# A projection slab moved between the channel transposes, the state product put first on GpSimd, and decays picked from split cumulative sums in a transformer-and-SSD kernel

## What is computed

```python
xbc = jax.nn.silu(causal_depthwise_conv(xbc, conv_w[l], conv_b[l]))
xs, bs, cs = jnp.split(xbc, [SSD_D_INNER, SSD_D_INNER + SSD_GROUPS * SSD_STATE], axis=-1)
dt = jax.nn.softplus(dt_raw + dt_bias[l]);  A = -jnp.exp(a_log[l])
...
x = xh * dt;  a_cs = jnp.cumsum(dt * A)
seg = a_cs[:, :, :, None] - a_cs[:, :, None, :]
decay = jnp.exp(jnp.where(causal, seg, -jnp.inf))
cb = jnp.einsum('bclgn,bcsgn->bclsg', Cc, Bc)
y_diag = jnp.einsum('bclsg,bclsgr,bcsgrp->bclgrp', cb, decay, x)
states = jnp.einsum('bclgn,bclgr,bclgrp->bcgrpn', Bc, decay_to_end, x)
y_off = jnp.einsum('bclgn,bcgrpn,bclgr->bclgrp', Cc, prev, jnp.exp(a_cs))
...
merged = sigmoid(gate_a) * (y_attn @ w_attn_branch[l]) + sigmoid(gate_b) * (y_ssd @ w_ssd_branch[l])
```

## Time and profile before

| | |
|---|---|
| median of 3 runs | 1382.62 us (1381.84 to 1382.67) |
| profiled execution, its own time | 1379.86 us |
| its span on the core | 1378.1 us |
| TensorE matmuls busy | 1324.7 us, 96% |
| weight loads (PEld) busy | 1206.4 us, 88% |
| VectorE, ScalarE, GpSimd busy | 944.8, 766.2, 205.6 us |
| mean granted clock of TensorE | 0.988 of full |

### The profile page before, as it was taken

One profiled execution on the slowest core, in us unless ns is written; L12 is line 12 of the kernel. 1 busy time (PEld: TensorE's weight loads), 2 busy tenths in 40 slices (PEclk: granted clock), 3 DMA queues, 4 the chain that ended last, 5 costly groups with the idle time before them and its releaser, 6 DMA issues.

```text
span 1378.1 us, 23083 instructions
## 1 busy us (share of the span) xinstructions
PE 1324.7 (96%) x9022; PEld 1206.4 (88%) x9022; DVE 944.8 (69%) x1369; ACT 766.2 (56%) x1150; POOL 205.6 (15%) x165
## 2 busy tenths in 40 slices
PE   9999999999989999999999998989999999999998
PEld 8999989889989999988998887979999788777876
DVE  6555575486566555566687775765666799999996
ACT  5333346565545333366465775325645677777774
POOL 1222220030001222210301313410001000202020
PEclk9999999999999999999999999999998999999999
DMA  8655544522356555544543442315455599999991
GB/s 311 212 187 186 186 142 157 183 93 93 131 156 197 183 183 184 171 135 154 184 148 123 123 154 71 100 47 180 143 169 184 212 400 365 339 367 334 370 338 52
DMA packets 73943, 263.44 MB, mean 191 GB/s; under 512 B 8320, under 2 KB 9600, under 8 KB 73728
## 3 DMA queue, kind: packets, MB, share of 16 engines
q1 hardware_dynamic: 72864, 260.39, 55.5%
q10 hardware_dynamic: 992, 1.86, 0.4%
HBM read 261.17 MB, written 1.05 MB: 190 GB/s over the span
## 4 chain that ended last, share of the span: by engine, by line
PE 69%; DVE 9%; ACT 5%; issue 2%; POOL 1%; DVEq 0%; ACTq 0%; POOLq 0%
PE bank L561 21%; PE bank L563 20%; PE bank L562 20%; DVE sb_wlo L518 3%; DVE sb_wlo L505 2%; ACT sb_Uh L636 1%; PE bank L2782 1%; PE bank L653 1%; ACT sb_aw L1729 1%; PE bank L2839 1%; DVE sb_XC L2118 1%; PE bank L741 1%; ACT sb_whi L489 0%; POOL sb_Xe L2441 0%; ACT sb_XC L1762 0%
## 5 line engine op out<-in xcount | busy, mean ns | idle before, releaser
L505 DVE TENSOR_TENSOR sb_wlo<-sb_raw,sb_whi 128x1024 fp32r<-128x1024 f32 (+2 forms) x304 | 384.0, 1308 | 166.3 <-ACT sb_whi L489 166.1
L489 ACT ACTIVATE sb_whi<-sb_raw 128x1024 fp32r<-128x1024 f32 (+3 forms) x308 | 301.9, 1030 | 227.8 <-PE bank L563 221.7
L561 PE MATMUL bank<-sb_Uh,sb_whi 128*128 128x256 f32 x1216 | 348.8, 287 | 11.5 <-DVE sb_wlo L505 4.3
L562 PE MATMUL bank<-sb_Ul,sb_whi 128*128 128x256 f32 x1216 | 345.3, 284 | 0.0
L563 PE MATMUL bank<-sb_Uh,sb_wlo 128*128 128x256 f32 x1216 | 345.1, 284 | 0.0
L561 PEld LDWEIGHTS bank<-sb_Uh,sb_whi 128*128 128x128 f32 x1216 | 234.1, 192 | 16.6 <-issue 9.2
L562 PEld LDWEIGHTS bank<-sb_Ul,sb_whi 128*128 128x128 f32 x1216 | 234.2, 193 | 0.9
L563 PEld LDWEIGHTS bank<-sb_Uh,sb_wlo 128*128 128x128 f32 x1216 | 234.2, 193 | 0.0
L561 PE MATMUL bank<-sb_whi,sb_Uh 128*128 128x256 f32 (+3 forms) x560 | 161.1, 288 | 7.1 <-DVE sb_Ul L645 5.3
L563 PE MATMUL bank<-sb_whi,sb_Ul 128*128 128x256 f32 (+3 forms) x560 | 158.5, 283 | 0.0
L562 PE MATMUL bank<-sb_wlo,sb_Uh 128*128 128x256 f32 (+3 forms) x560 | 158.5, 283 | 0.0
(11 more groups left out here) (407 smaller groups left out, 2258.5 us busy)
## 6 DMA issues: line engine op xcount, KB each, us to landing
sb_raw<-in_slabs SPq DMA_DIRECT2D x162, 512.0 KB, 4.5
sb_raw<-in_ffn_in SPq DMA_DIRECT2D x88, 512.0 KB, 4.5
sb_raw<-in_moe_in SPq DMA_DIRECT2D x50, 512.0 KB, 5.7
sb_raw<-in_ffn_out SPq DMA_DIRECT2D x44, 512.0 KB, 3.9
sb_raw<-in_moe_out SPq DMA_DIRECT2D x26, 512.0 KB, 5.8
sb_deep_free<-in_moe_in SPq DMA_DIRECT2D x16, 512.0 KB, 5.9
sb_deep_uh<-in_moe_in SPq DMA_DIRECT2D x16, 512.0 KB, 5.2
sb_deep_ul<-in_moe_in SPq DMA_DIRECT2D x16, 512.0 KB, 6.3
```

Of the source, the lines that this page charges most:

```text
L489: nc.scalar.activation(whi[:, i % NSLOT, c], raw[:, i % NSLOT, c], ACT.Copy).then_inc(S("hi_done"), 1)
L505: nc.vector.tensor_tensor(wlo[:, i % NSLOT, c], raw[:, i % NSLOT, c], whi[:, i % NSLOT, c].bitcast(F32), ALU.subtract).then_inc(S("lo_done ...
L561: pe.matmul(o, lh, rh, start=start, stop=False, skip_group_check=True)
L562: pe.matmul(o, lh, rl, start=False, stop=False, skip_group_check=True)
```

## The change

The six parts, as the code has them:

1. Decays. VectorE spreads dt*A over a tile DTR with the 32 heads four times side by side; two matmuls with `upto` (new, `cst_mm`) give the cumulative sums with heads along the partitions, four copies of them, in bank 4. VectorE casts them to fp32r (CST) and turns the second and fourth copy into the remainder. Rows 0 to 63 and rows 64 to 127 each hold high and low part of all heads. A decay row is now one fp32r matmul of 64 rows: a 0/1 column PICKR, spread over 128 columns, times CST. The two banks' matmuls alternate between the row halves.
2. The slab of u = 0 goes between the second and third block of transposes (`side(0)`), B's transposes go ahead of the blocks, and inside the loop pass u now has slab u + 1 (up to u = 4).
3. ScalarE casts slab wa2 after the third Silu, and makes the decays `ee` before the XS copies; BTM is copied after two of them.
4. VectorE does the remainder of that slab before `fe`.
5. GpSimd starts a unit when its own two blocks of XS are there, and makes Xe before Xd.
6. Xd, Xe and BTM no longer share their place with XC.

```diff
+        ("pick", (np.arange(P)[:, None] % SH == np.arange(SH)[None, :]) * 1.0),
...
+                    hi_upto("wa0")
...
             act.activation(ssm[:, 9], ssm[:, 5], ACT.Exp).then_inc(S("ee"), 1)
-            hi_upto("wa0")
+            for j in range(8):
+                if j == 2:
+                    act.wait_ge(*reach("bt_tr", 1))
+                    act.activation(BTM[:].rearrange("p g n -> p (g n)"), bank[4][:, :], ACT.Copy).then_inc(S("bt_ev"), 1)
+                act.wait_ge(*reach("xs_tr", j + 1))
+                act.activation(XS[:, :, j * 256:(j + 1) * 256], tok(j % 4, 256), ACT.Copy).then_inc(S("xs_ev"), 1)
...
+            side_out(0)
             for u in range(8):
-                if u < 6:
-                    hi_upto(f"wa{u}" if u < 4 else f"g{u}")
+                if u < 5:
+                    hi_upto(f"wa{u + 1}" if u < 3 else f"g{u + 1}")
...
-                if u < 6:
-                    side_out(u)
+                if u < 5:
+                    side_out(u + 1)
...
+                    dve.tensor_copy(DTR[:], ssm[:, 2:4].unsqueeze(2).to_broadcast([P, NT, P // SH, SH])).then_inc(S("dt_d"), 1)
...
+            dve.tensor_copy(PICKR[:], const("pick")).then_inc(S("cst"), 1)
+            dve.wait_ge(*reach("cst_mm", 1))
+            dve.tensor_copy(CST[:], bank[4][:, 0:T]).then_inc(S("cst"), 1)
+            dve.wait_ge(*reach("cst", 2))
+            for r in (SH, 3 * SH):
+                dve.tensor_tensor(CST[r:r + SH, :], bank[4][r:r + SH, 0:T], CST[r:r + SH, :].bitcast(F32), ALU.subtract).then_inc(S("cst"), 1)
...
+            lo_upto("wa0")
             dve.wait_ge(*reach("ee", 1))
             dve.tensor_tensor(ssm[:, 7], ssm[:, 7], ssm[:, 0], ALU.mult).then_inc(S("fe"), 1)
-            lo_upto("wa0")
...
-                pool.wait_ge(*reach("xs_ev", 8))
+                pool.wait_ge(*reach("xs_ev", 2 * g + 2))
...
+            claim(4, "cst", 4)
+            for t in range(NT):
+                last = pe.matmul(bank[4][:, t * P:(t + 1) * P], DTR[:, t].rearrange("p a h -> p (a h)"), const("upto"),
+                                 start=t == 0, stop=True, skip_group_check=True)
+            last.then_inc(S("cst_mm"), 1)
...
+            xs_turn(0)
+            xs_turn(1)
+            pe.wait_ge(*reach("dsa_olo", 8))
+            side(0)
+            for j in range(2, 8):
+                xs_turn(j)
             for u in range(9):
...
-                        for h in range(4):
-                            col = ssm[:, 2 + t, 8 * g + 4 * k + h:8 * g + 4 * k + h + 1].to_broadcast([P, P])
-                            last = pe.matmul(bank[n % 4][:, h * P:(h + 1) * P], col, const("upto"), start=h == 0, stop=True,
-                                             skip_group_check=True)
+                    for h in range(4):
+                        for k in range(2):
+                            rows, hd = slice(64 * k, 64 * k + 64), 8 * g + 4 * k + h
+                            last = pe.matmul(bank[(2 * u + k) % 4][:, h * P:(h + 1) * P], PICKR[rows, hd:hd + 1].to_broadcast([64, P]),
+                                             CST[rows, t * P:(t + 1) * P], start=h == 0, stop=True, skip_group_check=True)
...
-                    if u < 6:
+                    if u < 5:
+                        side(u + 1)
```

More of the change, by code:

```diff
@@ L348, in two_blocks @@
             pad = sb("pad", [P, P], F32, p2)
+            CST = sb("CST", [P, T], F32R, p2)
+            PICKR = sb("PICKR", [P, SH], F32R, p2)
+            DTR = sb("DTR", [P, NT, P // SH, SH], F32, p2)
+            Xd = sb("Xd", [P, 2, 512], F32, p2)
+            Xe = sb("Xe", [P, 512], F32, p2)
+            BTM = sb("BTM", [P, SG, SN], F32, p2)
             with ExitStack() as pa:
@@ L359, in two_blocks @@
                 ST = sb("ST", [P, SG, 512], F32, pa)
-                Xd = sb("Xd", [P, 2, 512], F32, pa)
-                Xe = sb("Xe", [P, 512], F32, pa)
-                BTM = sb("BTM", [P, SG, SN], F32, pa)
             with ExitStack() as pa:
@@ L1764, in _ @@
                     gate2_out(3)
-            for j in range(8):
-                act.wait_ge(*reach("xs_tr", j + 1))
-                act.activation(XS[:, :, j * 256:(j + 1) * 256], tok(j % 4, 256), ACT.Copy).then_inc(S("xs_ev"), 1)
-            act.wait_ge(*reach("bt_tr", 1))
-            act.activation(BTM[:].rearrange("p g n -> p (g n)"), bank[4][:, :], ACT.Copy).then_inc(S("bt_ev"), 1)
+                    hi_upto("wa0")
             act.preload_act_table(ACT.Exp)
@@ L2205, in _ @@
                     t, g = divmod(u, 4)
-                    if u < 6:
-                        lo_upto(f"wa{u}" if u < 4 else f"g{u}")
+                    if u < 5:
+                        lo_upto(f"wa{u + 1}" if u < 3 else f"g{u + 1}")
                     for k in range(2):
@@ L2721, in _ @@
             gate2(3)
-            pe.wait_ge(*reach("dt_d", 2))
+            pe.wait_ge(*reach("dt_d", 3))
             claim(5, "acs", 1)
@@ L2737, in _, with side, xs_turn @@
                 last.then_inc(S("cb_mm"), 1)
-            for j in range(8):
+            def side(u):
+                s_ = need(f"wa{u}" if u < 4 else f"g{u}")
+                claim(7, "side_ev", u + 1)
+                src = (OAh, OAl) if u < 4 else (Uh, Ul)
+                by_feature(s_, 7, *src, KD, 256).then_inc(S("slab_used"), 1)
+            def xs_turn(j):
                 pe.wait_ge(*reach("xc", 3 + j // 2))
```

22 lines of the change are left out of this document (10 added, 12 removed).

## The result

| | before | after |
|---|---|---|
| median of 5 runs (lowest to highest) | 1382.67 us (1381.84 to 1387.41) | 1374.99 us (1374.81 to 1376.87) |
| profiled execution, its span | 1379.86, 1378.1 us | 1376.87, 1375.1 us |
| first cumulative sum, z0, the stretch between | 823.84, 918.79, 94.95 us | 829.93, 912.07, 82.14 us |

The ratio is 0.9943, 95% interval [0.9925, 0.9961]: 0.6% faster, 7.7 us. 1366.0 was forecast, in a range of 1361 to 1373, and the measured time lies above it. The sign was right, the size half of what was said.

A forecast was written before the change was run, and what follows sets the result against it. TensorE, busy 96% of the span, bounds the kernel, apart from its waits and low clock. Decays 8.5, waits 6.2, clock 2.3 and added work -0.45 make 16.6 us saved: 1366.0 us, range 1361.0 to 1373.0.

The forecast's parts named there:

- The end: Loop's last three passes: waits for VectorE of 1.6, 2.6 and 2.8 us, low clock only for the last 4.86 us.
- the end gives it back: Rival: clock falls at the first of three end waits, costing 4 to 5 us; saving 12, 1370.6 us; chance 0.10.
- my 78.36: Forecast length in us from the first cumulative sum, 823.84, to slab z0's start, 902.2; before, 94.95.
- At nothing: Items put at no cost: the DTR copy in the top-k rounds, the loads, 32 more constant columns, everything behind z0.
- The wait for Xe and the slow stretch behind it: Before the first state product: wait of 4.7 us goes, and 5.1 us at low clock with it, worth 2.3 us.
- ST comes late once: Pass 1: TensorE waits 0.9 us because bank 6 is emptied late and ST's copy ends only at 845.7.
- The move itself: Slab wa0 among the transposes really runs earlier; the rival that it is held up: about 7 saved, 1375.6 us, chance 0.04.
- the decay pass: Each of eight decay passes on TensorE: 0.70 us instead of 1.76, saving 8.5 us in all, bounds 4.8 and 10.5.
- the nearest row: Trace row behind the 0.70 us: 64-row weight loads on alternating halves, starting about 0.05 us apart.
- my estimate of 0.86 us: Decay pass by the skill's formula: eight weight loads of 107 ns; the sum would then save 1.3 us less.
- what the decays are worth: Shorter decays on TensorE's line: 8 x (1.76 - 0.70) = 8.5 us saved, added sums costing 0.45.
- longer waits of the end: Waits for VectorE in the loop's last three passes, within the 7.9 us of waits left after the change.

The follow-up runs named there:

- warm-end run: Kernel after, plus matmuls on zeros before the three waits for VectorE's bank-6 product at the loop's end: 1368.95 us, ratio 0.9891.
- best version: Kernel after, with VectorE's bank-6 product placed earlier and 8 matmuls on zeros behind the product with ST: 1365.28 us; with the constants table not widened, 1364.74.
- S alone: Kernel before, with only the slab moved among the transposes and the copies made earlier; old decays, Xd first: 1377.01 us, ratio 0.9964.
- D alone: Kernel before, with only the new 64-row fp32r decays and their transposed sums: 1388.36 us, ratio 1.0036.
- D with S: Kernel after, with GpSimd making Xd before Xe again, so new decays and moved slab only: 1384.50 us, ratio 1.0005.
- X: GpSimd making Xe before Xd; as the only edit to the kernel before: 1376.40 us, ratio 0.9959.
- the first run above: Kernel before, unchanged, run and traced again as a control: 1383.44 us, ratio 1.0001.

## Why the prediction was right and wrong

The miss is 1374.99 - 1366.0 = 9.0 us. Two steps failed, and each is measured by a run that undoes it.

**"The end", 4.5 us.** The step "TensorE's line: ... last bank-6 product at 897.3, and from there 4.86 us at the low clock as today" put the fall at the last of three waits. It came at the first, and the rival "the end gives it back" is what happened, down to its size: 4 to 5 us forecast, 3.9 in the stretch (82.21 against my 78.36), some 1.2 in z0, where the clock is low for 4.8 us instead of the 2.3 of the first trace before, and 4.5 in the warm-end run. I gave it 0.10 on one trace, in which the clock had held through 2.62 us. The same program run again let it fall there. Of four traces with the old end (the kernel before twice, and with 32 and 64 unread columns) the clock held past the first wait in two and fell in it or right behind it in two; in all five traces with the change's end and without zeros (first waits of 2.43 and once 1.52 us) it fell there. One execution did not carry that step; without other traces the rival deserved about the forecast's chance.

**"At nothing", about 3 us.** "The 32 further constant columns ride on one early load" looked at the transfer alone. The columns move tiles, and the matmuls that read them go from 227.8 to 232.3 ns: 3.0 us by the traces, and by the medians 3.7 in the kernel before, 3.0 in the kernel after and 0.5 in the best version. That all before the stretch would stay as it was I took for granted, without a line on it.

These make about 7.5 of the 9.0; the rest is within the spread of these runs (the kernel after run again had a median of 1373.46).

**Right: up to 56.9 us into the stretch.** Forecast was the last decays before the end at 880.4 - 823.84 = 56.6; they start at 56.87. The wait for Xe and the slow stretch behind it are gone; Xe is ready in every pass; ST comes late once, 1.27 us for my 0.9. The move itself is real: S alone gives 5 to 6 us. With the clock held the whole stretch is 77.50, for my 78.36. That is nearer than its parts deserve: it holds no fall of the clock at all, where I had kept 4.86 us at the low level, so an error the other way is hidden in it, of which ST's wait is 0.4 us.

**Right in kind, a little too long: the decay pass.** A pass takes 0.59 us, not 0.70, and for the reason that I gave: the halves run beside each other. The alternating order, by which I chose the nearest row, isn't needed: they pair up when issued in turn too. The four pairs start 0.16, 0.11 and 0.11 us apart, and the product comes 0.20 behind the last pair, so the two changes of array shape cost about 0.05 and 0.09 where I had 2 x 0.10 and a bit for the head. Of the two rules of the Trainium skill that I weighed, the drain of TensorEngine Tiling (Key Properties) is no larger here than that 0.14 us in both changes. The load time of TensorE: Matmul & The Clock Gate (LDWEIGHTS), 107 ns by its formula whatever the rows, agrees with the loads of one half, which start 0.11 us apart; my estimate of 0.86 us came from counting eight of them where four stand behind each other.

**Mis-sized: what the decays are worth.** I took it from "every microsecond taken from TensorE's line shortens the loop". That holds only for the passes in which TensorE is the bound: 4.3 us with the clock held, 1.9 without, and 4.8 us lost with the slab moved and Xd first. The sum as a whole counted part of that, in its longer waits of the end.

**Not in the prediction at all:** that the parts depend on each other. I summed their savings. D alone gains nothing in its stretch, D with S undoes half of what S gives there, and X, which I valued at two waits, is worth 6 to 7 us alone and 11 inside the change.

## What to carry to other kernels

Before making one engine faster, look at what it will wait for then: a longer wait costs its own length and the clock behind it, so a cheaper instruction in front of a wait can make a kernel slower. Where TensorE must wait for another engine for several short passes, compare the chain with the clock held by matmuls on zeros; if that is faster, the clock was the cost. An added constant is a move of every tile behind it: compare the pace of untouched loops in both traces before explaining the rest. And two traces of one program can differ by more than the effect sought: 94.6 to 97.1 us for the same stretch here, so trace the kernel before more than once.

## What was not expected of the hardware

- The 512-column matmuls with hh and hl follow each other every 228 or 232 ns according to where the tiles behind the constants start; two of three offsets, 256 bytes apart, were fast, the one between slow.
- The clock fell behind a wait of 2.4 to 2.6 us in some executions and held through the same wait in others of the same program (the earlier trace rows against the first run above).
- Eight 64-row matmuls of 128 columns take 0.59 us, in pairs of one upper and one lower half 0.11 us apart, also when four of one half are issued before the four of the other; 128-row fp32 ones take 0.22 each.
- One GpSimd multiplication of the same shape takes 1.04 us or 2.02, a microsecond apart; the slow ones ran beside a VectorE pass over 128x1024 values.
